# 128 instead of 96 stationary columns in the matmuls of an expert layer, and its bias in four groups of 32 rows

## The chip, the cores and the metric

The kernel runs on one core of a Trainium2 chip. The metric is device time in microseconds (us) of one execution, from the first to the last instruction plus what little lies around them; lower is better. The engines are TensorE (PE, with its weight loads listed apart as PEld), VectorE (DVE), ScalarE (ACT), GpSimd (POOL) and SyncE (SP), which here only issues DMAs.

## The reference

One encoder layer on 512 tokens of width 1024 in float32: three attention mixers with gates, then a mixture of experts with 32 experts of which each token takes four, then a final norm. The change touches the experts alone. What they compute, cut to what matters:

```
def expert_block(args):
    xb, e = args
    gu = xb @ w_gu[e] + b_gu[e]                       # 1024 -> 2048
    g = jnp.minimum(gu[:, :D_EXPERT], SWIGLU_LIMIT)
    lin = jnp.clip(gu[:, D_EXPERT:], -SWIGLU_LIMIT, SWIGLU_LIMIT)
    act = g * jax.nn.sigmoid(SWIGLU_ALPHA * g) * (lin + 1.0)
    return act @ w_down[e] + b_down[e]                # 1024 -> 1024
```

## The kernel before, in words

**Precision.** Large products are made of float32 values split in two fp32r parts, high and low. `A @ B` is then three matmuls: high x high, low x high, high x low.

**First part (0 to about 424 us).** Norm, projection, attention, gates and the output product. Its products (`gemm`, whose matmuls are recorded at L1440 to L1442) hold 128x128 stationary tiles and stream 512 columns. Then the router picks experts, and the 2048 token choices are packed into jobs. A job is one expert and up to 96 slots (`SLOTS = 96`); there are 32 jobs in this execution.

**Job loop (about 433 to 1580 us).** Each job has two products. `gate_up` has 8 weight parts of 1 MB; for each, 12 matmuls with the tokens' transposed chunk `xt_hi[:, k, :]` or `xt_lo[:, k, :]` (128 rows, 96 columns) as stationary operand and 512 columns of weights streaming into PSUM banks 0 to 3 (L1743 with the high weights `h_w`, L1746 with the low ones `l_w`). `down` has 4 weight parts, with 12 matmuls each, from `at_hi` and `at_lo` into banks 4 and 5 (L1761, L1766). Every matmul loads its stationary operand anew. So a job has 96 + 48 = 144 such matmuls. Between them stand 8 transposes of the activation (`turn_act`, in the second part of the next job's `gate_up`), 8 of the tokens to come (`turn_tokens`, after the first part of `down`), both recorded at L1467, and the bias.

**The bias of the first matrix.** It opens `gate_up` with four matmuls (L1735), one for each bank: a stationary operand `expert_gu` [96, 96] in bf16 that is one in the rows of the job's expert, and `bias_gu` [96, 2048] in bf16, which holds the bias of the 32 experts as three bf16 parts in three groups of 32 rows. POOL makes these parts after the attention (L941 to L959), and the first job's `expert_gu` just before that job (L992, L994); later ones are written by ACT (L839).

**Who feeds whom.** The parts of weights pass through 12 buffers `a_w`. SP loads a part when TensorE is through with the part 12 before it (L591, L594). ACT rounds `a_w` to `h_w` (L817; 8 buffers, so it waits for the part 8 before), and DVE subtracts to get `l_w` (L1190), in the buffer of `a_w`. DVE also makes `xt_lo` (L1329) and `at_lo` (L1334) and does most of the activation. The jobs' experts are read from a table, and the loop runs over pairs of jobs. The order on each engine is written out by hand; semaphores tie the engines.

**End.** `down_biases` (L1814) adds the second matrix' bias in float32, its stationary operand `gate_t` taken in groups of 32 rows; `last_rows` (L1818) adds the last job's rows with the 128-column stationary operands `token_hot`.

Of the kernel before, what the change touches and what calls it, by code (L numbers as in the profile page):

```python
# [102 lines left out]
def encoder_kernel(nc, x, mem, norm_mix, w_in, q_norm_a, k_norm_a, sink_b, norm_mem, w_mem_kv,  # L103
# [3 lines left out]
    with ctx:  # L107
# [40 lines left out]
        bias_f = sb("bias_f", [96, D], F32, 188 * KIB)  # L148
# [49 lines left out]
        bias_gu = sb("bias_gu", [96, 2 * D], BF16, 202 * KIB)  # L198
# [27 lines left out]
        blocks_end = small("blocks_end", [P, 3, N_EXP], F32)  # L226
        blocks_start = small("blocks_start", [P, 3, N_EXP], F32)
        job_ge = small("job_ge", [96, NJ], F32)
        job_lt = small("job_lt", [96, NJ], F32)
        job_hot = small("job_hot", [96, NJ], F32)  # L230
# [26 lines left out]
        at_hi = sb("at_hi", [P, KD, SLOTS], F32R, 174 * KIB)  # L257
        at_lo = sb("at_lo", [P, KD, SLOTS], F32R, 177 * KIB)
# [16 lines left out]
        job_hot_b = small("job_hot_b", [96, NJ], BF16)  # L275
        expert_gu = small("expert_gu", [96, SLOTS], BF16)
# [378 lines left out]
        def _(act):  # L655
# [181 lines left out]
            def name_gu(j):  # L837

                nc.scalar.activation(expert_gu[:], job_hot_b[:, bass.ds(j, 1)].to_broadcast([96, SLOTS]), ACT.Copy).then_inc(expert_gu_ready, 1)  # L839

            def take_xt(j):
                act.wait_ge(x_ps, j + 1)
                nc.scalar.activation(xt_hi[:].rearrange("p (h k) m -> p h (k m)", h=2), of_two_banks(6), ACT.Copy).then_inc(xt_hi_done, 1)

            def take_act(j):
                act.wait_ge(at_ps, j + 1)
                nc.scalar.activation(at_hi[:].rearrange("p (h k) m -> p h (k m)", h=2), of_two_banks(6), ACT.Copy).then_inc(at_hi_done, 1)
# [86 lines left out]
        def _(pool):  # L934
# [6 lines left out]
            bias_pieces = [(bias_gu[:, 0:D], b_gate_up[0][:, 0:D]), (bias_gu[:, D:2 * D], b_gate_up[0][:, D:2 * D])]  # L941
            pool.wait_ge(y_ps, STEPS)
            for n, (part, bias) in enumerate(bias_pieces):
                for g in range(3):
                    pool.dma_start(bias_f[N_EXP * g:N_EXP * (g + 1), :], bias).then_inc(bias_in, 16)
                pool.wait_ge(bias_in, 48 * (n + 1))

                def to_parts(rows):
                    step.link(nc.gpsimd.tensor_copy(part[rows, :], bias_f[rows, :]))

                def take_off(rows):
                    step.link(nc.gpsimd.tensor_tensor(bias_f[rows, :], bias_f[rows, :], part[rows, :], ALU.subtract))

                to_parts(slice(0, 96))
                for lo in (32, 64):
                    take_off(slice(lo, lo + 32))
                    to_parts(slice(lo, lo + 32))
                take_off(slice(64, 96))
                to_parts(slice(64, 96))  # L959
# [85 lines left out]
        def _(dve):  # L1045
# [230 lines left out]
            for g in range(3):  # L1276
# [4 lines left out]
            dve.wait_ge(blocks_ready, 3)  # L1281
# [4 lines left out]
            step.inc(nc.vector.tensor_tensor(job_ge[:], counter[0:96, 0:NJ], ps[0:96, 1, P:P + NJ], ALU.is_ge))  # L1286
# [574 lines left out]
```

## Time and profile before

| | |
|---|---|
| time, median of 3 runs | 1604.47 us (1602.7 to 1605.66) |
| time of the profiled execution | 1600.28 us |
| its span, first to last instruction | 1598.4 us |
| mean granted TensorE clock | 0.997 of 2.4 GHz |
| PE busy | 1566.0 us, 98% of the span |
| DVE busy | 1283.4 us, 80% |
| ACT busy | 1084.7 us, 68% |
| POOL busy | 432.0 us, 27% |

Busy time of PE is made of matmuls whose ends are modelled and overlap, so how fast it goes is read from the starts of matmuls, not from their durations. A row of the timeline that ends in x4 stands for four instructions in a row; the next row's start minus its own, divided by four, is the spacing. "Idle before" is time an engine had nothing to run, with what it waited for.

### The profile page before, as it was taken

To read this page: it belongs to the slowest core of one execution; us is meant where nothing else is said; L and a number is where in the kernel's file an instruction comes from. 1 tells how busy PE (TensorE), PEld (TensorE's weight loads), DVE (VectorE), ACT (ScalarE), POOL (GpSimd) and SP (SyncE) were. 2 spreads that over 40 slices of the span, in tenths; PEclk is the share of its full clock that TensorE was granted. 3 is DMA by queue.
4 is the path that set the end of the run, shared out by engine and by line. 5 is a ranking of instruction groups with operands and counts; after the bars stand their busy time and mean duration, and the time that the engine had idled before them with its cause. 6 is when DMAs were issued, how large, how long until landed. Compare 5 with 4: busy or idle time off the path is not lost.

```text
span 1598.4 us, 21810 instructions
## 1 busy us (share of the span) xinstructions
PE 1566.0 (98%) x7654; PEld 1139.1 (71%) x7654; DVE 1283.4 (80%) x1019; ACT 1084.7 (68%) x999; POOL 432.0 (27%) x265
## 2 busy tenths in 40 slices
PE   8999999999899999999999999999999999999997
PEld 7866688888766777777777777777777777777774
DVE  3768734337699989999898899998988999999984
ACT  6368723224477778777777787777777877777772
POOL 0000260000033622324432222344332223443220
PEclk9999999999999999999999999999999999999999
DMA  7310022337399999999999999999999999999983
GB/s 270 111 59 21 11 86 84 128 119 290 122 381 346 365 367 379 368 369 376 358 369 370 370 381 368 372 369 360 367 369 372 363 377 368 368 363 373 375 298 125
DMA packets 102566, 466.97 MB, mean 292 GB/s; under 512 B 13289, under 2 KB 13825, under 8 KB 69729
## 3 DMA queue, kind: packets, MB, share of 16 engines
q1 hardware_dynamic: 94416, 448.71, 73.5%
q0 software_dynamic: 7776, 17.68, 5.2%
q8 instruction: 24, 0.39, 0.1%
q10 hardware_dynamic: 336, 0.08, 0.0%
q14 instruction: 14, 0.11, 0.0%
HBM read 456.82 MB, written 19.27 MB: 298 GB/s over the span
## 4 chain that ended last, share of the span: by engine, by line
PE 91%; DVE 6%; issue 1%; DMA 1%; ACT 0%; POOL 0%; DVEq 0%; ACTq 0%; POOLq 0%
PE ps L1743 28%; PE ps L1761 14%; PE ps L1746 14%; PE ps L1766 7%; PE ps L1440 6%; PE ps L1442 6%; PE ps L1441 6%; PE ps L1467 4%; DVE l_w L1190 2%; PE ps L1735 2%; PE ps L1593 1%; DVE head_max L1119 1%; PE ps L1549 1%; DVE probs L1137 1%; PE ps L1476 0%
## 5 line engine op out<-in xcount | busy, mean ns | idle before, releaser
L1190 DVE TENSOR_TENSOR l_w<-a_w,h_w 128x2048 fp32r<-128x2048 f32 x384 | 865.4, 2290 | 31.0 <-ACT h_w L817 29.1
L817 ACT ACTIVATE h_w<-a_w 128x2048 fp32r<-128x2048 f32 x384 | 731.1, 1914 | 234.5 <-PE ps L1746 169.2
L965 POOL TENSOR_TENSOR mark_sb<-ones 1x1 f32<-1x1 f32 x93 | 245.9, 2644 | 718.6 <-ACT y_sb L865 708.5
L1743 PE MATMUL ps<-h_w,xt_hi 128*96 128x512 f32 x1024 | 286.7, 401 | 2.3 <-DVE xt_lo L1329 2.3
L1743 PE MATMUL ps<-h_w,xt_lo 128*96 128x512 f32 x1024 | 278.3, 393 | 0.0
L1746 PE MATMUL ps<-l_w,xt_hi 128*96 128x512 f32 x1024 | 277.9, 393 | 0.0
L1743 PEld LDWEIGHTS ps<-h_w,xt_lo 128*96 128x96 f32 x1024 | 165.6, 162 | 71.5
L1746 PEld LDWEIGHTS ps<-l_w,xt_hi 128*96 128x96 f32 x1024 | 165.2, 161 | 71.1
L1743 PEld LDWEIGHTS ps<-h_w,xt_hi 128*96 128x96 f32 x1024 | 163.3, 162 | 70.6 <-ACT h_w L817 1.7
L1761 PE MATMUL ps<-h_w,at_hi 128*96 128x512 f32 x512 | 162.1, 398 | 0.2 <-issue 0.2
L1761 PE MATMUL ps<-h_w,at_lo 128*96 128x512 f32 x512 | 159.5, 392 | 0.0
L486 DVE TENSOR_TENSOR w_low<-w_raw,w_high 128x2048 fp32r<-128x2048 f32 (+2 forms) x36 | 69.0, 1953 | 112.0 <-ACT w_high L478 112.0
L1766 PE MATMUL ps<-l_w,at_hi 128*96 128x512 f32 x512 | 139.0, 393 | 0.0
L1440 PE MATMUL ps<-w_high,h_hi 128*128 128x512 f32 x352 | 138.1, 392 | 0.6 <-DVE mem_lo L1065 0.5
L1442 PE MATMUL ps<-w_high,h_lo 128*128 128x512 f32 x352 | 137.1, 390 | 0.0
L1441 PE MATMUL ps<-w_low,h_hi 128*128 128x512 f32 x352 | 137.0, 389 | 0.0
L1761 PEld LDWEIGHTS ps<-h_w,at_lo 128*96 128x96 f32 x512 | 82.6, 161 | 36.1
L1766 PEld LDWEIGHTS ps<-l_w,at_hi 128*96 128x96 f32 x512 | 82.6, 161 | 35.9
L1761 PEld LDWEIGHTS ps<-h_w,at_hi 128*96 128x96 f32 x512 | 80.2, 162 | 32.1 <-issue 1.0
L971 POOL DMA_INDIRECT xg<-h_rows,gather_row x32 | 88.0, 2749 | 7.1 <-issue 5.4
L785 ACT ACTIVATE gate_sb<-ps,row_rstd 128x512 f32<-128x512 f32 x24 | 16.6, 690 | 105.7 <-PE ps L1442 105.7
L1440 PEld LDWEIGHTS ps<-w_high,h_hi 128*128 128x128 f32 x352 | 66.1, 188 | 15.1 <-DVE mem_lo L1065 0.8
(247 smaller groups left out, 1555.6 us busy)
## 6 DMA issues: line engine op xcount, KB each, us to landing
a_w<-in_w_gate_up SPq DMA_DIRECT2D x256, 1024.0 KB, 7.0
a_w<-in_w_down SPq DMA_DIRECT2D x128, 1024.0 KB, 6.6
w_raw<-in_w_in SPq DMA_DIRECT2D x8, 2048.0 KB, 8.0
w_raw<-in_w_out SPq DMA_DIRECT2D x2, 2048.0 KB, 7.6
w_raw<-in_w_in SPq DMA_DIRECT2D x2, 1024.0 KB, 7.8
x_sb<-in_x SPq DMA_DIRECT2D x8, 256.0 KB, 7.3
w_raw<-in_w_mem_kv SPq DMA_DIRECT2D x1, 2048.0 KB, 11.2
x<-in_x SPq DMA_DIRECT2D x4, 512.0 KB, 5.2
```

The lines of the kernel that those rows point to most:

```text
L486: nc.vector.tensor_tensor(wl[u % 2][:, a * COLS:b * COLS], raw[u % 2][:, a * COLS:b * COLS], wh[u % 2][:, a * COLS:b * COLS].bitcast(F32), ...
L817: nc.scalar.activation(h_w[m % H_SLOTS][:], a_w[m % A_SLOTS][:], ACT.Copy).then_inc(wh_done, 1)
L965: nc.gpsimd.tensor_tensor(mark_sb[:], ones[0:1, 0:1], ones[0:1, 0:1], ALU.mult).then_inc(marked, 1)
L971: nc.gpsimd.indirect_dma_start(out=xg[s][:], out_offset=None, in_=h2_rows, in_offset=bass.IndirectOffsetOnAxis(ap=rows, axis=0), bounds_ch ...
L1190: nc.vector.tensor_tensor(l_w[m % A_SLOTS][:], a_w[m % A_SLOTS][:], h_w[m % H_SLOTS][:].bitcast(F32), ALU.subtract).then_inc(wl_done, 1)
L1440: nc.tensor.matmul(bank, hi, w_hi, start=start, stop=False)
L1441: nc.tensor.matmul(bank, hi, w_lo, start=False, stop=False)
L1442: return nc.tensor.matmul(bank, lo, w_hi, start=False, stop=stop)
L1743: nc.tensor.matmul(ps[0:SLOTS, n, :], x_part[:, k, :], w_h[:, n * COLS:(n + 1) * COLS], start=False, stop=False)
L1746: last = nc.tensor.matmul(ps[0:SLOTS, n, :], xt_hi[:, k, :], w_l[:, n * COLS:(n + 1) * COLS], start=False, stop=k == KD - 1)
L1761: nc.tensor.matmul(ps[0:SLOTS, 4 + n, :], a_part[:, 2 * q + k, :], w_h[:, (2 * k + n) * COLS:(2 * k + n + 1) * COLS], start=q == 0 and k = ...
L1766: last = nc.tensor.matmul(ps[0:SLOTS, 4 + n, :], at_hi[:, 2 * q + k, :], w_l[:, (2 * k + n) * COLS:(2 * k + n + 1) * COLS], start=False, s ...
```

## The change

Every stationary operand of the job loop's matmuls gets 128 columns. A helper, `chunk`, takes them from a tile in which high and low part lie one after the other (`xt`, `at_both`): the 96 columns of chunk k and the first 32 of what follows it. The matmul writes all 128 partitions of its bank; partitions 96 to 127 hold sums that nobody reads, as the readers still take `ps[0:SLOTS]`. Only the very last chunk of the low part has nothing behind it, and stays at 96 columns (4 matmuls a job in `gate_up`, 2 in `down`). The bias becomes two fp32r tiles [128, 512], high and low, in which row group n (32 experts) holds the columns of bank n; `expert_gu` is [128, 128] in fp32r, and each bank takes one matmul of 32 rows from each tile: eight matmuls instead of four. Some preparing steps go from three groups to four.

```
-        bias_f = sb("bias_f", [96, D], F32, 188 * KIB)
+        bias_f = sb("bias_f", [P, COLS], F32, 188 * KIB)
-        bias_gu = sb("bias_gu", [96, 2 * D], BF16, 202 * KIB)
+        bias_hi = sb("bias_hi", [P, COLS], F32R, 202 * KIB)
+        bias_lo = sb("bias_lo", [P, COLS], F32R, 204 * KIB)
-        xt_hi = sb("xt_hi", [P, KD, SLOTS], F32R, 160 * KIB)
-        xt_lo = sb("xt_lo", [P, KD, SLOTS], F32R, 163 * KIB)
+        xt = sb("xt", [P, 2, KD * SLOTS], F32R, 160 * KIB)
+        xt_hi, xt_lo = (xt[:, n, :].rearrange("p (k m) -> p k m", k=KD) for n in range(2))
...
-        expert_gu = small("expert_gu", [96, SLOTS], BF16)
+        expert_gu = small("expert_gu", [P, P], F32R)
...
-            for n, (part, bias) in enumerate(bias_pieces):
-                for g in range(3):
-                    pool.dma_start(bias_f[N_EXP * g:N_EXP * (g + 1), :], bias).then_inc(bias_in, 16)
-                pool.wait_ge(bias_in, 48 * (n + 1))
...
+            for n in range(4):
+                pool.dma_start(bias_f[N_EXP * n:N_EXP * (n + 1), :], b_gate_up[0][:, n * COLS:(n + 1) * COLS]).then_inc(bias_in, 16)
+            pool.wait_ge(bias_in, 64)
+            step.link(nc.gpsimd.tensor_copy(bias_hi[:], bias_f[:]))
+            step.link(nc.gpsimd.tensor_tensor(bias_lo[:], bias_f[:], bias_hi[:].bitcast(F32), ALU.subtract))
...
-            step.link(nc.gpsimd.memset(expert_gu[:], 0.0))
-            for g in range(3):
-                nc.gpsimd.memset(expert_gu[N_EXP * g:N_EXP * g + 1, :], 1.0).then_inc(first_expert, 1)
-            pool.wait_ge(first_expert, 3)
+            step.link(nc.gpsimd.memset(expert_gu[:].bitcast(F32), 0.0))
+            for n in range(4):
+                nc.gpsimd.memset(expert_gu[N_EXP * n:N_EXP * n + 1, :].bitcast(F32), 1.0).then_inc(first_expert, 1)
+            pool.wait_ge(first_expert, 4)
...
-            for g in range(3):
+            for g in range(TB):
                 step.inc(nc.vector.tensor_tensor_scan(blocks_end[:, g, :], ones[:, 0:N_EXP], blocks[:], 0.0, ALU.mult, ALU.add))
...
+            def chunk(both, part, k):
+
+                w = SLOTS if part and k == KD - 1 else P
+                at = (part * KD + k) * SLOTS
+                return both[:].rearrange("p a m -> p (a m)")[:, at:at + w], w
...
-                for n in range(4):
-                    nc.tensor.matmul(ps[0:SLOTS, n, :], expert_gu[:], bias_gu[:, n * COLS:(n + 1) * COLS], start=True, stop=False)
+                for part in (bias_hi, bias_lo):
+                    for n in range(4):
+                        rows = slice(N_EXP * n, N_EXP * (n + 1))
+                        nc.tensor.matmul(ps[:, n, :], expert_gu[rows, :], part[rows, :], start=part is bias_hi, stop=False)
...
-                    for x_part in (xt_hi, xt_lo):
+                    for part in range(2):
+                        x_part, rows = chunk(xt, part, k)
                         for n in range(4):
-                            nc.tensor.matmul(ps[0:SLOTS, n, :], x_part[:, k, :], w_h[:, n * COLS:(n + 1) * COLS], start=False, stop=False)
+                            nc.tensor.matmul(ps[0:rows, n, :], x_part, w_h[:, n * COLS:(n + 1) * COLS], start=False, stop=False)
                     wait_low(pe, i, m)
                     for n in range(4):
-                        last = nc.tensor.matmul(ps[0:SLOTS, n, :], xt_hi[:, k, :], w_l[:, n * COLS:(n + 1) * COLS], start=False, stop=k == KD - 1)
+                        last = nc.tensor.matmul(ps[:, n, :], chunk(xt, 0, k)[0], w_l[:, n * COLS:(n + 1) * COLS], start=False, stop=k == KD - 1)
```

`down` is changed as `gate_up` is. Two places are shown as the engines' programs have them. The first is on TensorE, in the loop's body, at the seam where a `down` ends and the next `gate_up` begins with its bias. A number behind a name is its buffer; the last figures are the partitions and columns that are written. Before:

```order
L1761 MATMUL ps<-h_w_179,at_hi 96x512 x2
L1761 MATMUL ps<-h_w_179,at_lo 96x512 x2
L1766 MATMUL ps<-l_w_171,at_hi 96x512 x4
L1733 REGISTER_ALU
L1735 MATMUL ps<-bias_gu,expert_gu 96x512 x4
L534 REGISTER_ALU
L1743 MATMUL ps<-h_w_180,xt_hi 96x512 x4
L1743 MATMUL ps<-h_w_180,xt_lo 96x512 x4
```

And the same place of the changed kernel (high and low part are now one tile, so both read `at_both` or `xt`):

```order
L1759 MATMUL ps<-h_w_180,at_both 128x512 x6
L1759 MATMUL ps<-h_w_180,at_both 96x512 x2
L1764 MATMUL ps<-l_w_172,at_both 128x512 x4
L1727 REGISTER_ALU
L1731 MATMUL ps<-bias_hi,expert_gu 128x512 x4
L1731 MATMUL ps<-bias_lo,expert_gu 128x512 x4
L535 REGISTER_ALU
L1740 MATMUL ps<-h_w_181,xt 128x512 x8
L1743 MATMUL ps<-l_w_173,xt 128x512 x4
```

Nothing moved: the bias' four matmuls became eight, and all but the last two of the high weights' eight write 128 partitions.

The second place is on POOL, just ahead of the first gathering of tokens for the job loop (`xg` is the tile of gathered tokens, `h_rows` the rows in memory). Before:

```order
L987 MEMSET mark_sb 1x1
L989 MEMSET xg_186 96x1024
L989 MEMSET xg_187 96x1024
L992 MEMSET expert_gu 96x96
L994 MEMSET expert_gu 1x96 x3
L971 DMA xg_186<-h_rows,gather_row 96x1024
```

After:

```order
L975 MEMSET mark_sb 1x1
L977 MEMSET xg_186 96x1024
L977 MEMSET xg_187 96x1024
L980 MEMSET expert_gu 128x128
L982 MEMSET expert_gu 1x128 x4
L959 DMA xg_186<-h_rows,gather_row 96x1024
```

The gathering stands behind one memset more, and the first of them is larger.

## Rows read from the trace of the kernel before

**Rows 1.** Busy us (count): PE, PEld, DVE, ACT, POOL; then clock, DMA share, GB/s
```profile
520.00:1540.00 1020.00, 1020.00 (x4721) 719.56 (x4720) 924.75 (x491) 794.43 (x547) 357.01 (x204) 1.00 0.99 369
```

**Rows 2.** Waits in 600 to 1400 us: total, times, longest
```profile
SPq L591 <- PE ps L1746: 396.2, 179, 2.8
```

**Rows 3.** The chain that ended last: start, length, what
```profile
1204.26 1.85 PE ps L1761 x8
1239.72 1.85 PE ps L1761 x8
```

**Rows 4.** Timeline of PE around the first `gate_up` product within the loop
```profile
504.03 1.16 PE L1743 MATMUL ps<-h_w,xt_hi 128*96 128x512 f32 x4 [1.28 <-DVE xt_lo L1329]
```

**Rows 5.** Timeline of PE in the job loop: start, length, what
```profile
903.13 1.09 PE L1743 MATMUL ps<-h_w,xt_hi 128*96 128x512 f32 x4
...
916.07 1.09 PE L1746 MATMUL ps<-l_w,xt_hi 128*96 128x512 f32 x4
...
927.82 1.09 PE L1766 MATMUL ps<-l_w,at_hi 128*96 128x512 f32 x4
928.75 1.03 PE L1735 MATMUL ps<-bias_gu,expert_gu 96*96 96x512 bf16 x4
...
930.54 1.08 PE L1743 MATMUL ps<-h_w,xt_lo 128*96 128x512 f32 x4
```

**Rows 6.** Timeline of PE in the first part's products
```profile
257.78 0.39 PE L1442 MATMUL ps<-w_high,h_lo 128*128 128x512 f32 x1
...
261.86 0.39 PE L1442 MATMUL ps<-w_high,h_lo 128*128 128x512 f32 x1
...
377.08 0.40 PE L1441 MATMUL ps<-w_low,h_hi 128*128 128x512 f32 x1
...
378.70 0.39 PE L1442 MATMUL ps<-w_high,h_lo 128*128 128x512 f32 x1
...
379.38 0.39 PE L1442 MATMUL ps<-w_high,h_lo 128*128 128x512 f32 x1
```

**Rows 7.** Timeline of PE at the end of the kernel
```profile
1572.12 0.62 PE L1761 MATMUL ps<-h_w,at_hi 128*96 128x512 f32 x2
...
1579.53 1.09 PE L1766 MATMUL ps<-l_w,at_hi 128*96 128x512 f32 x4
1580.54 1.98 PE L1814 MATMUL ps<-down_bias,gate_t 32*128 32x512 f32 x4
1582.45 1.66 PE L1818 MATMUL ps<-y_hi_last,token_hot 96*128 96x512 f32 x6
1583.95 1.52 PE L1818 MATMUL ps<-y_lo_last,token_hot 96*128 96x512 f32 x6
```

**Rows 8.** Weight loads by form: count, busy us, mean ns, idle before
```profile
L1743 PEld LDWEIGHTS ps<-h_w,xt_hi 128*96 128x96 f32 x1024 | 163.3, 162 | 70.6 <-ACT h_w L817 1.7 <-DVE xt_lo L1329 1.5 <-issue 0.2
L1440 PEld LDWEIGHTS ps<-w_high,h_hi 128*128 128x128 f32 x352 | 66.1, 188 | 15.1 <-DVE mem_lo L1065 0.8 <-DVE h_lo L1160 0.3 <-issue 0.2
```

**Rows 9.** Timeline around `down_biases((0, 1))`: PE, and the weight loads
```profile
1566.11 1.09 PE L1766 MATMUL ps<-l_w,at_hi 128*96 128x512 f32 x4
1567.13 1.99 PE L1814 MATMUL ps<-down_bias,gate_t 32*128 32x512 f32 x8
1567.13 0.30 PEld L1814 LDWEIGHTS ps<-down_bias,gate_t 32*128 32x128 f32 x4 [0.39 <-issue]
1567.66 0.19 PEld L1814 LDWEIGHTS ps<-down_bias,gate_t 32*128 32x128 f32 x2 [0.24 <-issue]
1568.09 0.19 PEld L1814 LDWEIGHTS ps<-down_bias,gate_t 32*128 32x128 f32 x2 [0.24 <-issue]
```

**Rows 10.** Timeline of POOL and PE ahead of the job loop
```profile
427.32 0.62 POOL L994 MEMSET expert_gu<- 1x96 bf16 x3
428.84 1.04 POOL L971 DMA_INDIRECT xg<-h_rows,gather_row  x1 [0.90 <-POOL expert_gu L994]
433.02 0.88 PE L1467 MATMUL ps<-ident,xg 96*128 96x96 f32 x8 [1.50 <-DMA xg<-h_rows,gather_row]
```

More of the change, by code:

```diff
@@ L225, in encoder_kernel @@
         blocks = small("blocks", [P, N_EXP], F32)
[L226 to L230, printed above, removed]
+        blocks_end = small("blocks_end", [P, TB, N_EXP], F32)
+        blocks_start = small("blocks_start", [P, TB, N_EXP], F32)
+        job_ge = small("job_ge", [P, NJ], F32)
+        job_lt = small("job_lt", [P, NJ], F32)
+        job_hot = small("job_hot", [P, NJ], F32)
         place = small("place", [P, TB, N_EXP], F32)
@@ L251, in encoder_kernel @@
         h_w = [sb(f"h_w{i}", [P, 2 * D], F32R, at * KIB) for i, at in enumerate((0, 8, 16, 24, 128, 136, 112, 120))]
-        xt_hi = sb("xt_hi", [P, KD, SLOTS], F32R, 160 * KIB)
-        xt_lo = sb("xt_lo", [P, KD, SLOTS], F32R, 163 * KIB)
+        xt = sb("xt", [P, 2, KD * SLOTS], F32R, 160 * KIB)
+        xt_hi, xt_lo = (xt[:, n, :].rearrange("p (k m) -> p k m", k=KD) for n in range(2))
         xg = [sb(f"xg{i}", [SLOTS, D], F32, (166 + 4 * i) * KIB) for i in range(2)]
-        at_hi = sb("at_hi", [P, KD, SLOTS], F32R, 174 * KIB)
-        at_lo = sb("at_lo", [P, KD, SLOTS], F32R, 177 * KIB)
+        at_both = sb("at_both", [P, 2, KD * SLOTS], F32R, 174 * KIB)
+        at_hi, at_lo = (at_both[:, n, :].rearrange("p (k m) -> p k m", k=KD) for n in range(2))
         sg_sb = sb("sg_sb", [SLOTS, D], F32, 180 * KIB)
@@ L837, in name_gu @@
             def name_gu(j):
[L839 removed]
+                nc.scalar.activation(expert_gu[:], job_hot_b[:, bass.ds(j, 1)].to_broadcast([P, P]), ACT.Copy).then_inc(expert_gu_ready, 1)
             def take_xt(j):
                 act.wait_ge(x_ps, j + 1)
[L843 removed]
+                nc.scalar.activation(xt_hi.rearrange("p (h k) m -> p h (k m)", h=2), of_two_banks(6), ACT.Copy).then_inc(xt_hi_done, 1)
             def take_act(j):
                 act.wait_ge(at_ps, j + 1)
[L847 removed]
+                nc.scalar.activation(at_hi.rearrange("p (h k) m -> p h (k m)", h=2), of_two_banks(6), ACT.Copy).then_inc(at_hi_done, 1)
             def sigmoid(j, between=None):
@@ L1272, in _ @@
             step.link(nc.vector.tensor_scalar(blocks[:, 0:1], blocks[:, 0:1], 1.0, None, ALU.max))
-            for g in range(3):
+            for g in range(TB):
                 step.inc(nc.vector.tensor_tensor_scan(blocks_end[:, g, :], ones[:, 0:N_EXP], blocks[:], 0.0, ALU.mult, ALU.add))
             dve.wait_ge(dve_chain, step.n)
-            for g in range(3):
+            for g in range(TB):
                 nc.vector.tensor_tensor(blocks_start[:, g, :], blocks_end[:, g, :], blocks[:], ALU.subtract).then_inc(blocks_ready, 1)
             step.inc(nc.vector.tensor_scalar(job_table[0:1, 1, 1:2], blocks_end[0:1, 0, N_EXP - 1:N_EXP], 0.5, -0.75, ALU.mult, ALU.add))
-            dve.wait_ge(blocks_ready, 3)
+            dve.wait_ge(blocks_ready, TB)
             step.link(nc.vector.scalar_tensor_tensor(out=place[:], in0=blocks_start[:, 0:1, :].to_broadcast([P, TB, N_EXP]), scalar=float(SLOTS),
@@ L1758, in down @@
                     for k in range(2):
-                        for a_part in (at_hi, at_lo):
+                        for part in range(2):
+                            a_part, rows = chunk(at_both, part, 2 * q + k)
                             for n in range(2):
-                                nc.tensor.matmul(ps[0:SLOTS, 4 + n, :], a_part[:, 2 * q + k, :], w_h[:, (2 * k + n) * COLS:(2 * k + n + 1) * COLS],
-                                                 start=q == 0 and k == 0 and a_part is at_hi, stop=False)
+                                nc.tensor.matmul(ps[0:rows, 4 + n, :], a_part, w_h[:, (2 * k + n) * COLS:(2 * k + n + 1) * COLS],
+                                                 start=q == 0 and k == 0 and part == 0, stop=False)
                     wait_low(pe, i, m)
@@ L1765, in down @@
                         for n in range(2):
-                            last = nc.tensor.matmul(ps[0:SLOTS, 4 + n, :], at_hi[:, 2 * q + k, :], w_l[:, (2 * k + n) * COLS:(2 * k + n + 1) * COLS],
+                            last = nc.tensor.matmul(ps[:, 4 + n, :], chunk(at_both, 0, 2 * q + k)[0], w_l[:, (2 * k + n) * COLS:(2 * k + n + 1) * COLS],
                                                     start=False, stop=q == DN_PARTS - 1 and k == 1)
```

27 lines of the change are left out of this document (8 added, 19 removed).

## The prediction

> **What bounds the kernel now.** I read the stretches first. From 520 to 1540 us TensorE is busy all of the time, at full clock, while DVE is busy 924.75 of 1020 us (91%), ACT 794 us (78%) and the DMA engines nearly always (0.99, 369 GB/s) [rows 1]. Three candidates, then: PE, DVE and DMA. The waits decide against DMA: SP, which issues the loads, waited 396 us of the 800 from 600 to 1400 for TensorE to free a buffer, and for the `gate_up` parts alone [rows 2]. Loads are held back by PE, not PE by loads. The chain that ended last shows PE repeating itself every 35.46 us (1239.72 - 1204.26) [rows 3]; that is one job. DVE needs 0.907 x 35.46 = 32.2 us of it, ACT 27.6 us. So PE sets the pace from 504 us on. Before that it does not: at 504.03 it still waits 1.28 us for DVE's `xt_lo` [rows 4], since DVE is catching up with its `l_w` there. What PE saves in the first two jobs is lost in that wait; about 30.5 of the 32 jobs count (30 whole ones and the last `down`).
>
> How fast PE goes is read from starts. From 903.13 to 916.07 us there are 14 groups of four: 12.94 / 56 = 231.1 ns a matmul, with 96 stationary columns and 512 streamed [rows 5]. In the first part of the kernel the same kind of matmul, fp32r, 512 streamed columns, a new weight load each, but 128 stationary columns, starts every 4.08 / 18 = 226.7 ns (257.78 to 261.86) [rows 6]. So a wider stationary operand goes with a shorter spacing, by 4.4 ns.
>
> Is it the columns? The two stages differ in other things. First, DVE, ACT and DMA work beside the job loop. But the last `down` keeps 7.41 / 32 = 231.6 ns from 1572.12 to 1579.53, when the loads and the splitting of weights are over [rows 7]. Second, the job loop changes its bank with each matmul, while `gemm` stays in one. But the final matmuls L1818 (128 columns of `token_hot`) also change bank each time, and the six from 1583.95 last 1.52 us, which less the 0.39 us of one is 1.13 / 5 = 226 ns [rows 7]. What is left is the columns.
>
> The short spacing is not there at once. After transposes, `gemm` starts with seven at 1.62 / 7 = 231.4 ns (377.08 to 378.70) and only then goes to 0.68 / 3 = 226.7 ns [rows 6]. With 96 columns it doesn't come in 56 in a row [rows 5].
>
> **The change, part by part.**
>
> *The 144 matmuls of a job.* PE is disturbed at four places: bias, two sets of transposes, and the matmuls that stay at 96 columns. I take seven long spacings behind each of the first three (21), the 4 narrow ones in `gate_up` and seven behind them (11), the 2 narrow ones in `down` with the four up to the next bias (6): 38 keep 231 ns and 106 gain 4.3 ns. That is -0.456 us a job. Bounds: all 144 gain, -0.62 us; none, 0.
>
> *Longer weight loads.* A load of 128 columns takes 188 ns, one of 96 takes 162 [rows 8]. In a stream it is covered by the matmul before it (over 220 ns). Where a full operand is loaded behind transposes, which last under 100 ns each, it isn't: 26 ns twice a job, +0.05 us. Bounds 0 and +0.1.
>
> *The bias.* Now, from 927.82 to 930.54 us there are four L1766, the four bias matmuls and four L1743: 2.72 us, and less eight at 0.231 the bias costs 0.87 us a job [rows 5]. After: eight matmuls, each of 32 rows, in four row groups of the array. No row shows fp32r in this form; the nearest is `down_biases` in float32. With one row group, two matmuls (four records, since float32 takes two each) last 1.98 us [rows 7]; with two row groups, four matmuls (eight records) last 1.99 us, and their loads come in twos, four loads of about 0.18 us within 0.30 us [rows 9]. So different row groups run beside each other. With four groups I expect two rounds of 0.227 us and some 0.02 for their staggered starts, 0.48 us. But such a switch costs time. On the way in, 1.02 us pass from 1566.11 to 1567.13 for four matmuls that take 0.92: +0.10 [rows 9]. Within the form, a float32 round takes 0.43 us (loads at 1567.66 and 1568.09 [rows 9]); from 1580.54 to 1582.45 there are four rounds, 1.72 us, but 1.91 us pass: +0.19, a first load that nothing covers and a drain at the end [rows 7]. And the six L1818 from 1582.45 take 1.50 instead of 1.36 us: +0.14, of which 0.03 are the long first spacings that I counted already [rows 7]. Together 0.48 + 0.10 + 0.19 + 0.11 = 0.88 us, and for two more groups' loads at the start I take 0.91: +0.04 us a job. Bounds: no switching cost, 0.48 - 0.87 = -0.39; no overlap of the row groups, 8 x 0.227 + 0.43 - 0.87 = +1.38 (with all the switching).
>
> On weight loads the Trainium skill speaks against this form ("TensorE: Matmul & The Clock Gate", LDWEIGHTS): the time goes by the columns, P / 1.2 ns, so 32 rows cost as much as 128. The durations agree in slope (32 columns more, 26 ns more [rows 8]). Eight loads of 128 columns in a row would by that page be an estimated 0.85 us, as much as the old bias in all; but it also says that loads of different row groups overlap, and [rows 9] show it for two.
>
> *Ahead of the loop.* POOL writes the first `expert_gu` (three memsets, 0.62 us together) and then gathers the first tokens, for which PE waits 1.50 us [rows 10]. One memset more (0.2 us) and a larger first one (128x128 float32 for 96x96 bf16) put the gathering back by 0.3 us, and nothing takes it up, as DVE and PE both start from it. One more scan and one more subtraction on DVE lie beside this wait. +0.3 us once. Bounds 0 and 0.6.
>
> *At nothing:* making the bias' parts, on POOL, shorter than before and long ahead of its first use; SP waits for it only ahead of loads that wait for the merging too. If that cover were gone it would be a gain. ACT writes a larger `expert_gu` (0.3 us of ACT, which has 7.9 us a job free). The partitions 96 to 127 written in vain cost no streamed column. DVE, DMA and ACT do what they did; a job of 35.1 instead of 35.46 us asks 1% more of each, and DVE's 32.2 us fit.
>
> **Sum.** A job: -0.456 + 0.05 + 0.04 = -0.37 us. Times 30.5: -11.2 us; with +0.3 us: -10.9 us. The profiled execution, 1600.28 us, would come to 1589.4 us; it ran 4.2 us under the median of the runs shown, so against that 1604.47 the forecast is 1593.5 us. From no change this measurement can tell about 0.2%, 3.2 us.
>
> **The rivals.**
>
> *The short spacing never comes in the job loop.* The seven long spacings behind each disturbance are there, and something that I did not see keeps the others long too. Then 0.05 + 0.04 = +0.09 us a job and +0.3: +3 us, 1607.5 us. For it: L1818 shows only five short spacings with changing banks. Against: nothing else differs.
>
> The Trainium skill would have this (same page, Back-to-back issue gap): N / 2.4 + 2.5 ns, 215.8 ns for 512 streamed columns, whatever the stationary operand has. The trace disagrees, with 231.1 and 226.7 ns [rows 5, 6].
>
> *The four row groups do not overlap.* This is the other side. Place: the eight bias matmuls at the head of each `gate_up`. Price +1.38 us a job instead of +0.04, so 30.5 x (-0.456 + 0.05 + 1.38) = +29.7 us, 1634 us. It decides from the point where the bias takes 0.41 us more than now (1.28 us). For it: two groups were seen, never four, and never in fp32r. Against: [rows 9]. Overlap by halves, two and two, would be 0.93 us with 0.43, +0.49 a job, +3 us in all, within the first rival's range.
>
> *Switching costs nothing.* The loads of a 32-row group are hidden as others are, -0.39 us a job: 30.5 x (-0.456 + 0.05 - 0.39) = -24.3 us, 1580.5 us. For it: the four matmuls ahead of the present bias, which has 96 of 128 rows, pass in 0.93 us, without a gap [rows 5]. Against: each switch to 32 rows in [rows 7, 9].
>
> *DMA becomes the bound.* The engines are at 0.99, and the gain would stop where it begins: 1604 us. Against: [rows 2].
>
> **How the numbers follow.** Forecast 0.58, with its own range 1586 to 1600 us (all matmuls gain, or half of the 106); never short, or two and two, 0.17, about 1607; no overlap 0.09, 1634; switching free 0.13, 1580; DMA 0.03. Leaving out the 1634 case and the far ends of the others, the range is 1579 to 1608 us. Faster: 0.58 + 0.13 = 0.71. Same: half of the 0.17 case and more, and DMA, 0.15. Slower: 0.14.
>
> **What would show it.** In the changed kernel's timeline of the job loop: spacings near 226.7 ns from the eighth matmul behind transposes on (if 231 stays, the first rival); one job shorter than 35.46 by about 0.37 us; from the last `down` group's start to the second group of `gate_up`, 2.76 instead of 2.72 us (4.1: no overlap; 2.3: free switching); the matmuls at 96 columns followed by some of 231 ns; PE's wait ahead of the first transposes later by 0.3 us. The sum would be wrong above all if the narrow matmuls disturb nothing (then nearer -0.45 us), or if with four groups the switch costs other than with two.

## The result, and the profile after

The changed kernel is slower: 1610.56 us (median of 6 runs, 1609.28 to 1611.8) against 1603.93 us for the kernel before beside it (6 runs, 1602.49 to 1605.66), a ratio of 1.0043 with an interval of 1.0032 to 1.0054. The forecast was 1593.5 us and faster. The profiled execution of the changed kernel took 1609.7 us, with a span of 1607.9 us.

The page's busy times and the job loop's stretch in the changed kernel (busy us and count of PE, PEld, DVE, ACT, POOL; then clock, DMA share, GB/s), beside [rows 1]:

```profile
PE 1575.7 (98%) x7782; PEld 1253.5 (78%) x7782; DVE 1278.7 (80%) x1021; ACT 1085.7 (68%) x999; POOL 394.6 (25%) x252
520.00:1540.00 1020.00, 1020.00 (x4805) 814.17 (x4804) 919.93 (x488) 791.68 (x543) 347.38 (x203) 1.00 0.98 368
```

The waits of 600 to 1400 us, beside [rows 2] (total, times, longest):

```profile
SPq L592 <- PE ps L1743: 393.1, 177, 2.9
```

And the chain of work that ended last, beside [rows 3] (start, length, what):

```profile
1140.39 1.90 PE ps L1759 x8
...
1176.02 1.90 PE ps L1759 x8
```

The structure is the same: in this stretch PE is never idle and runs at full clock, and SP waits for it as long as before. But DVE, ACT and DMA do a little less in the same stretch, since a job now takes 1176.02 - 1140.39 = 35.63 us instead of 35.46. From the starts of all complete jobs between 600 and 1500 us the means are 35.644 us (25 jobs) and 35.460 us (26 jobs of before): +0.184 us, times 30.5 jobs +5.6 us. So the loss lies inside the jobs, on PE.

The timeline of PE in the changed kernel, the same stretch of a `gate_up` as [rows 5] (start, length, what):

```profile
909.03 2.03 PE L1740 MATMUL ps<-h_w,xt 128*128 128x512 f32 x8
910.90 1.09 PE L1743 MATMUL ps<-l_w,xt 128*128 128x512 f32 x4
911.83 2.01 PE L1740 MATMUL ps<-h_w,xt 128*128 128x512 f32 x8
913.67 1.08 PE L1743 MATMUL ps<-l_w,xt 128*128 128x512 f32 x4
914.58 2.03 PE L1740 MATMUL ps<-h_w,xt 128*128 128x512 f32 x8
916.45 1.09 PE L1743 MATMUL ps<-l_w,xt 128*128 128x512 f32 x4
917.38 2.01 PE L1740 MATMUL ps<-h_w,xt 128*128 128x512 f32 x8
```

A weight part is 12 matmuls. The part from 909.03 takes 2.80 us (233 ns a matmul), the next 2.75 (229), the next 2.80 again (233). All have 128 columns. They alternate with the number of the chunk: these are k = 3, 4 and 5. The short spacing was to come from the eighth matmul on and stay; here it comes in every second part and is lost again. The single spacings, as means over the complete jobs of each trace (my own reckoning from the starts, in ns, in order):

```
changed, k odd  (3, 5):  241 232 231 232 228 230 232 241 232 231 232 233   sum 2796
changed, k even (4, 6):  236 224 231 236 228 232 231 227 227 227 227 232   sum 2757
before,  k odd  (3, 5):  230 236 228 232 230 236 228 232 230 236 228 232   sum 2779
before,  k even (4, 6):  228 229 231 232 228 229 231 232 228 229 231 233   sum 2761
```

Two things were in the trace of before, too, and I had not looked: a pattern that repeats every four matmuls, and that differs between odd and even chunks. Its timeline shows it in the parts k = 4 (from 905.91 us, 2.76 us) and k = 5 (from 908.67 us, 2.78 us):

```profile
905.91 1.08 PE L1743 MATMUL ps<-h_w,xt_hi 128*96 128x512 f32 x4
...
908.67 1.09 PE L1743 MATMUL ps<-h_w,xt_hi 128*96 128x512 f32 x4
...
911.45 1.08 PE L1743 MATMUL ps<-h_w,xt_hi 128*96 128x512 f32 x4
```

The mean of 231.1 ns in [rows 5] hides both.

The two profiles differ by 9.5 us in span, the medians by 6.6. Part of the rest is the granted clock: the changed kernel's profiled execution had it at 0.50 from 420.6 to 427.4 us and from 437.6 to 441.0 us, where that of before had 1.00. It isn't the change: the profile of run 6 below, which has the old bias and 96 columns, had 0.51 in the first of these stretches, and that of run 10, with the new bias, 1.00.

### The profile page after: what moved, and what is told of

Its sections match the earlier page's. It is cut to its first block, busy times and chain, and to the rows that moved or that the text cites. A ratio compares the mean times of both kernels' runs of the same rounds, so it can differ in the third digit from the quotient of the medians.

```text
span 1607.9 us, 22055 instructions
## 1 busy us (share of the span) xinstructions
PE 1575.7 (98%) x7782; PEld 1253.5 (78%) x7782; DVE 1278.7 (80%) x1021; ACT 1085.7 (68%) x999; POOL 394.6 (25%) x252
## 4 chain that ended last, share of the span: by engine, by line
PE 92%; DVE 5%; issue 1%; DMA 1%; ACT 0%; DVEq 0%; ACTq 0%; POOLq 0%
PE ps L1740 29%; PE ps L1759 14%; PE ps L1743 14%; PE ps L1764 7%; PE ps L1428 6%; PE ps L1430 6%; PE ps L1429 6%; PE ps L1455 4%; PE ps L1731 1%; DVE l_w L1178 1%; PE ps L1581 1%; DVE head_max L1107 1%; PE ps L1537 1%; DVE probs L1125 1%; PE ps L1658 1%
## 5 line engine op out<-in xcount | busy, mean ns | idle before, releaser
L1740 PE MATMUL ps<-h_w,xt 128*128 128x512 f32 (+1 forms) x2048 | 525.1, 398 | 3.1 <-DVE xt L1317 3.1
L1740 PEld LDWEIGHTS ps<-h_w,xt 128*128 128x128 f32 (+1 forms) x2048 | 378.7, 187 | 102.2 <-issue 11.5
L1743 PE MATMUL ps<-l_w,xt 128*128 128x512 f32 x1024 | 277.6, 393 | 0.0
L1759 PE MATMUL ps<-h_w,at_both 128*128 128x512 f32 (+1 forms) x1024 | 261.4, 397 | 0.2 <-issue 0.2
L1743 PEld LDWEIGHTS ps<-l_w,xt 128*128 128x128 f32 x1024 | 192.8, 188 | 44.2
L1759 PEld LDWEIGHTS ps<-h_w,at_both 128*128 128x128 f32 (+1 forms) x1024 | 188.6, 187 | 44.8 <-issue 1.0
L1764 PE MATMUL ps<-l_w,at_both 128*128 128x512 f32 x512 | 140.8, 397 | 0.0
L1764 PEld LDWEIGHTS ps<-l_w,at_both 128*128 128x128 f32 x512 | 96.4, 188 | 23.5
L1430 PEld LDWEIGHTS ps<-w_high,h_lo 128*128 128x128 f32 x352 | 66.1, 188 | 13.8
L1429 PEld LDWEIGHTS ps<-w_low,h_hi 128*128 128x128 f32 x352 | 66.1, 188 | 13.3
```

The costliest lines, as they stand in the source:

```text
L1429: nc.tensor.matmul(bank, hi, w_lo, start=False, stop=False)
L1430: return nc.tensor.matmul(bank, lo, w_hi, start=False, stop=stop)
L1740: nc.tensor.matmul(ps[0:rows, n, :], x_part, w_h[:, n * COLS:(n + 1) * COLS], start=False, stop=False)
L1743: last = nc.tensor.matmul(ps[:, n, :], chunk(xt, 0, k)[0], w_l[:, n * COLS:(n + 1) * COLS], start=False, stop=k == KD - 1)
L1759: nc.tensor.matmul(ps[0:rows, 4 + n, :], a_part, w_h[:, (2 * k + n) * COLS:(2 * k + n + 1) * COLS], start=q == 0 and k == 0 and part == 0, ...
L1764: last = nc.tensor.matmul(ps[:, 4 + n, :], chunk(at_both, 0, 2 * q + k)[0], w_l[:, (2 * k + n) * COLS:(2 * k + n + 1) * COLS], start=False ...
```

## Experiments

All ratios are against the kernel before, run beside the experiment. "Job" is the mean period of complete jobs between 600 and 1500 us of the profiled execution; before has 35.460 us. Bytes are counted from the start of the tile that holds the stationary operand.

The first question was what differs between odd and even chunks. In the changed kernel chunk k starts at 384 k bytes (96 columns of 4 bytes) and ends 512 bytes further on. So an even k ends at a multiple of 256 bytes, an odd one 128 bytes past one. Theory A: the place of the stationary operand in its tile sets the spacing. Theory B: the register arithmetic and the waits between the weight parts do. Rival C: the spacing is a side matter and the new bias makes the loss. I first took the start of the operand for the place that counts, and runs 1 and 4 were forecast by it. After run 4 there were two forms of A: A1, only the end counts; A2, start and end do.

### 1. The same 128 columns, taken from a multiple of 512 bytes

It multiplies by other columns of the tile than the right ones, and by just as many.

```
                 at = (part * KD + k) * SLOTS
+                at = at // 128 * 128
```

> The changed kernel, but each 128-column stationary operand of the job loop is read from the nearest lower multiple of 128 columns of its tile (so it multiplies by other columns than it should; only the place of the reads differs). Theory A (what disturbs the matmuls is where in SBUF the stationary operand starts: chunks of 96 columns begin at multiples of 384 bytes, and the parts with odd k, whose start is no multiple of 256 bytes, are those with spacings of 241 ns): the odd parts look like the even ones, 12 matmuls in 2757 ns instead of 2796, and a job comes to about 35.4 us or less instead of 35.64; if the settled 226.7 ns is then kept across the parts too, 35.1 us. Theory B (register arithmetic and register waits at the seam between parts disturb them): nothing changes, 35.64 us.

Measured: 1591.7 us (5 runs), ratio 0.993 [0.9917, 0.9943], a job 35.077 us. Nearly all spacings are 227 ns; longer ones are left in the last chunk, whose operand with the low part keeps 96 columns, and behind the bias and one set of transposes (ten and nine of them). The number of columns, the bias, the waits and the register arithmetic stayed, so this is theory A, and the gain that the forecast had named is there: -0.38 us a job, beside -0.37 forecast. That the same columns are now read more than once is a rival that run 8 settles.

### 2. The old bias with 128 columns

The changed kernel with the bias of before: bf16, three groups, four matmuls. Only its stationary operand is widened to 128 columns.

```
-        expert_gu = small("expert_gu", [P, P], F32R)
+        expert_gu = small("expert_gu", [96, P], BF16)
...
+                for n in range(4):
+                    nc.tensor.matmul(ps[:, n, :], expert_gu[:], bias_gu[:, n * COLS:(n + 1) * COLS], start=True, stop=False)
```

> 128 columns in the products, but the bias as before (four bf16 matmuls of 96 rows). Theory A and B alike: the bias block cost the same before and after (1330 ns from the last matmul ahead of it to the second one behind it, less two ordinary spacings), so a job stays at 35.64 us within 0.1 us, and the time within 3 us of the changed kernel's. Rival C (the eight 32-row matmuls are what made the kernel slower): a job goes back to 35.46 us, and the time to that of the kernel before.

Measured: 1608.0 us (8 runs), ratio 1.0037 [1.0023, 1.0051], a job 35.633 us, with the same pattern (241 233 231 232 at the head of the odd parts). The loss stays without the new bias.

### 3. The loop written out on PE

```
-            with pe.Fori(0, pairs_but_one) as i:
+            for i in range(15):
```

> The changed kernel with TensorE's loop over 15 pairs of jobs written out, so that its waits are on constants and no register arithmetic stands between the parts (the other engines keep their loops). Theory B: the disturbances at the seams go, most matmuls start every 226.7 ns, a job comes to 35.1 us, and the kernel is faster than before by 10 us. Theory A: the pattern by odd and even k stays, 35.64 us a job, no change in time.

Measured: 1608.46 us (5 runs), ratio 1.0035 [1.0022, 1.0047], a job 35.644 us. PE's timeline:

```profile
907.11 2.03 PE L1740 MATMUL ps<-h_w,xt 128*128 128x512 f32 x8
...
909.90 2.01 PE L1740 MATMUL ps<-h_w,xt 128*128 128x512 f32 x8
...
912.66 2.03 PE L1740 MATMUL ps<-h_w,xt 128*128 128x512 f32 x8
```

Again 2.79 and 2.76 us, with the loop's register arithmetic gone. Theory B falls.

### 4. Five forms in the first part of the kernel

The products of the first part stay in one bank, have no loop and little beside them. The kernel before, whose gate products take stationary operands of other width and place, for some output blocks u and the middle k. Their results are other values.

```
+        FORMS = {6: (96, 0), 8: (96, 32), 10: (P, 32), 12: (P, 64), 14: (96, 64)}
...
+                            hi_m, lo_m = (v[:].rearrange("p k m -> p (k m)")[:, at:at + w] for v in (hi, lo))
+                            last = three(ps[0:w, BANK[u] + t, :], hi_m, lo_m, h_w[:, k, :], l_w[:, k, :], False, False)
```

> The kernel before, with other forms of the stationary operand in the gate products of the first part, one form for each product (k = 1 to 6; other columns than it should, so the values differ): 128 columns starting at a multiple of 512 bytes (control), 96 columns at 512, 96 at 512 + 128 bytes, 128 at 512 + 128, 128 at 512 + 256, 96 at 512 + 256. There are no registers here and few waits. Theory A: 226.7 ns for the control and for 512 + 256, about 231 ns for starts at 512 + 128, whatever the width. If it is the width: 231 ns for the three with 96 columns. Theory B: 226.7 ns for all six.

PE's timeline, one stretch of nine spacings for each of four forms:

```profile
218.51 0.39 PE L1442 MATMUL ps<-w_high,h_hi 128*96 128x512 f32 x1
...
220.58 0.39 PE L1442 MATMUL ps<-w_high,h_hi 128*96 128x512 f32 x1
...
248.74 0.39 PE L1442 MATMUL ps<-w_high,h_hi 128*96 128x512 f32 x1
...
250.78 0.39 PE L1442 MATMUL ps<-w_high,h_hi 128*96 128x512 f32 x1
...
275.95 0.40 PE L1442 MATMUL ps<-w_high,h_hi 128*128 128x512 f32 x1
...
278.05 0.39 PE L1442 MATMUL ps<-w_high,h_hi 128*128 128x512 f32 x1
...
306.34 0.39 PE L1442 MATMUL ps<-w_high,h_hi 128*128 128x512 f32 x1
...
308.38 0.39 PE L1442 MATMUL ps<-w_high,h_hi 128*128 128x512 f32 x1
```

2.07, 2.04, 2.10 and 2.04 us for nine. The first and the last of a block's eight chunks (k = 0 and 7) keep the ordinary operand; the means here are of the 17 spacings between the 18 matmuls of k = 1 to 6 alone, over the blocks of each form:

```
columns  starts at  ends at (bytes past a multiple of 512)   spacing, ns
   96        0        384                                      230.0
   96      128          0                                      226.7
   96      256        128                                      230.0
  128      128        128                                      232.8
  128      256        256                                      226.7
```

The expectation, which went by the start, missed all three forms with 96 columns (short for 0 and 256, long for 128) and had the two with 128 right; by the width alone the second and the fourth would have been missed.

With 96 columns the spacing can be 226.7 ns, and with 128 it can be 232.8. It is short where the end is at a multiple of 256 bytes, though starts differ (128, 256, and 0 in the ordinary form of [rows 6]). That speaks for A1; A2 can't say why 96 columns from 128 bytes on are fast.

### 5. The kernel before, with 96 columns that begin at multiples of 512 bytes

It takes other columns than the right ones; each operand ends 128 bytes past a multiple of 256.

> The kernel before, 96 columns, each stationary operand starting at a multiple of 512 bytes and ending 384 bytes past it (other columns than it should). A1: no short spacings, 230.0 ns in the steady state, as in the forms run, and a job near 35.35 us. If it is the start that counts: 226.7 ns and 35.0 us.

Measured: 1599.05 us (10 runs), ratio 0.9973 [0.9963, 0.9983], a job 35.327 us. In the steady state the spacings are 231 232 228 229, mean 230.0: never 226.7, although each operand starts well aligned. So the even chunks of the kernel before, which end 384 bytes past a multiple of 768, have what their end asks for (2761 / 12 = 230.1). Its odd chunks end at a multiple of 256 and yet have 231.6; runs 6 and 7 bear on that.

### 6. The kernel before, with 96 columns that end at multiples of 512 bytes

```
+            def aligned(tile, k):
+                at = k * SLOTS // 128 * 128 + 32
+                return tile[:].rearrange("p k m -> p (k m)")[:, at:at + SLOTS]
```

> The kernel before, 96 columns, but each stationary operand starts 128 bytes past a multiple of 512 bytes and so ends at one (other columns than it should). A1: 226.7 ns between most matmuls, a job near 35.0 us, 0.99 of before. A2: 231 ns as before, 35.46 us.

Measured: 1591.59 us (4 runs), ratio 0.9923 [0.9903, 0.9943], a job 35.033 us. With 96 columns (again other ones) nearly the whole gain is there. PE's timeline, `gate_up` from the end of the activation's transposes on, and then `down` behind those of the tokens:

```profile
1005.22 1.13 PE L1747 MATMUL ps<-h_w,xt_hi 128*96 128x512 f32 x4
...
1008.01 1.07 PE L1747 MATMUL ps<-h_w,xt_hi 128*96 128x512 f32 x4
...
1018.89 1.07 PE L1747 MATMUL ps<-h_w,xt_hi 128*96 128x512 f32 x4
...
1024.33 0.82 PE L1467 MATMUL ps<-ident,xg 96*128 96x96 f32 x8
...
1026.85 1.09 PE L1770 MATMUL ps<-l_w,at_hi 128*96 128x512 f32 x4
...
1032.41 1.08 PE L1770 MATMUL ps<-l_w,at_hi 128*96 128x512 f32 x4
```

From 1008.01 to 1018.89 are 48 matmuls, 10.88 us, 226.7 ns. From 1026.85 to 1032.41, behind the tokens' transposes, are 24 in 5.56 us: 231.7 ns (230 236 228 233), with operands that end just as well, and it stays so to the end of `down`. That is the pattern of the odd chunks in the kernel before. Not every set of transposes brings it: behind those of the activation the second spacing is 227 ns already (1005.22 to 1008.01 are 2.79 us, one of 292 ns and eleven of 227). Behind those of the tokens the stream with 96 columns keeps it for all 36 matmuls that are left of `down`. A stream with 128 columns leaves it: after seven spacings in [rows 6], after nine at this place in run 8, and the changed kernel's even chunks after seven. That the odd chunks of the kernel before are slow by the same state, and come into it by the even ones ahead, is an inference from the like pattern, which run 7 supports.

### 7. Even chunks with 128 columns, odd ones with 96

The tiles of the changed kernel are kept. Now every operand ends at a multiple of 256 bytes, except the last chunk's with the low weights, which has 128 columns so that all rows of the bank are closed.

```
-                w = SLOTS if part and k == KD - 1 else P
+                w = P if k % 2 == 0 or close else SLOTS
```

> The changed kernel, with 128 columns only for the even chunks and 96 for the odd ones (128 again for the last low-weight matmuls of each product), so that each operand ends at a multiple of 256 bytes although the odd ones start 128 bytes off. Computes what the reference does. Theory A1 (it is the end of the operand that counts): nearly all matmuls at 226.7 ns, a job at 35.1 us, 0.993 of before. Theory A2 (both start and end have to be at multiples of 256 bytes): odd parts stay near 231 ns, a job about 35.4 us.

Measured: 1593.35 us (6 runs), ratio 0.994 [0.9922, 0.9957], a job 35.107 us. Spacings are 227 ns in even and odd parts alike. The exceptions are 241 233 231 232 in the closing matmuls that end 128 bytes off, ten spacings behind the bias and thirteen behind the tokens' transposes. An odd chunk begins 384 bytes past a multiple of 768, so begins as badly as before, and is fast: A1 holds, A2 falls. It is also the very operand of the kernel before, with 96 columns and the same place. There it has 231.6 ns and here 227, with fast even chunks ahead of it.

### 8. The chunks 128 columns apart

The changed kernel, with gaps of 32 columns between chunks (the tiles `xt` and `at_both` grow by 2 KiB each, POOL clears the gaps once, the readers and writers take strided views). Every operand then begins and ends at a multiple of 512 bytes, and all 144 have 128 columns.

```
+        xt = sb("xt", [P, 2, KD * P], F32R, 160 * KIB)
+        xt_hi, xt_lo = (xt[:, n, :].rearrange("p (k m) -> p k m", k=KD)[:, :, 0:SLOTS] for n in range(2))
...
+                return both[:, part, k * P:(k + 1) * P], P
```

> The changed kernel, with the chunks of xt and at_both 128 columns apart (512 bytes) instead of 96, so each chunk starts and ends at a multiple of 512 bytes; computes what the reference does. Theory A (the place of the stationary operand in its tile sets the spacing): as the run with rounded starts, nearly all matmuls at 226.7 ns, a job at about 35.1 us, time 0.993 of the kernel before. Rival: the gain with rounded starts came from reading the same columns again; then the spacing stays at 231 ns and the time at that of the changed kernel.

Measured: 1589.46 us (6 runs), ratio 0.9918 [0.9901, 0.9934]. It beats both kernels. Its timeline and its chain:

```profile
908.98 1.98 PE L1741 MATMUL ps<-h_w,xt 128*128 128x512 f32 x8
910.79 1.07 PE L1744 MATMUL ps<-l_w,xt 128*128 128x512 f32 x4
911.70 1.98 PE L1741 MATMUL ps<-h_w,xt 128*128 128x512 f32 x8
```

```profile
1127.99 1.87 PE ps L1760 x8
...
1162.99 1.87 PE ps L1760 x8
```

12 matmuls in 2.72 us, 226.7 ns; a job 35.00 us. Each operand has its own columns here, so the rival of run 1 falls. From the changed kernel it is -0.64 us a job. Run 1, which moves the reads alone, gives 0.57 of it; besides, this run has no narrow operand left, and other tiles stand elsewhere.

### 9. The same with the old bias

> Chunks 128 columns apart and operands of 128 columns, but the bias as before (four bf16 matmuls of 96 rows); computes what the reference does. The bias blocks cost 0.87 us a job in both forms, so a job at 35.0 us. With the new bias the ten matmuls behind it take 50 ns more than the short spacing in the run with chunks 128 apart, with the old one about 11 ns, which would make it 1 us faster at most, too little to be sure of; 0.992 of the kernel before. If the bias form mattered once the spacing is short, more than 0.1 us a job would show.

Measured: 1588.56 us (4 runs), ratio 0.9903 [0.9888, 0.9919], a job 34.987 us. The best figure, but not told apart from run 8.

### 10. The new bias alone, with 96 columns

> The new bias alone: eight matmuls of 32 rows, but all stationary operands with 96 columns as before. Theory A (the loss is from the 128-column operands of odd chunks, which end 128 bytes past a multiple of 256): a job at 35.46 to 35.50 us, no change in time that can be told (within 2 us of before). Rival C (the bias makes the loss): 35.64 us, +6 us.

Measured: 1600.8 us (12 runs), ratio 0.9986 [0.9977, 0.9996], a job 35.407 us, 0.05 less than before. That is a little less than the 35.46 to 35.50 expected. Rival C falls: the bias does not cost. With 96 columns the seam, from the last matmul ahead of the bias to the second one behind it, even takes 1.27 us, where it takes 1.33 in the kernels before and after. PE's timeline at the seam:

```profile
929.48 1.09 PE L1764 MATMUL ps<-l_w,at_both 128*96 128x512 f32 x4
930.50 0.48 PE L1731 MATMUL ps<-bias_hi,expert_gu 32*96 32x512 f32 x4
930.81 0.41 PE L1731 MATMUL ps<-bias_lo,expert_gu 32*96 32x512 f32 x4
931.14 2.09 PE L1740 MATMUL ps<-h_w,xt 128*96 128x512 f32 x8
933.07 1.09 PE L1743 MATMUL ps<-l_w,xt 128*96 128x512 f32 x4
```

### 11. Five more forms

As run 4, to try the rule at other widths.

```
+        FORMS = {6: (64, 0), 8: (64, 32), 10: (112, 16), 12: (112, 0), 14: (P, 16)}
```

> More forms of the stationary operand in the gate products of the first part, as in the first forms run (other columns than it should). The end rule: 64 columns from 0 (ends at 256 bytes): 226.7 ns; 64 columns from 128 bytes (ends at 384): about 230 ns; 112 columns from 64 bytes (ends at 512): 226.7 ns; 112 from 0 (ends at 448): above 226.7 ns; 128 columns from 64 bytes (ends at 576): above 226.7 ns. If it is the start together with the width, 112 columns from 64 bytes are as long as 128 from 64 bytes.

PE's timeline, nine spacings with 64 columns and nine with 112:

```profile
217.87 0.40 PE L1442 MATMUL ps<-w_high,h_hi 128*64 128x512 f32 x1
...
219.94 0.39 PE L1442 MATMUL ps<-w_high,h_hi 128*64 128x512 f32 x1
...
275.50 0.39 PE L1442 MATMUL ps<-w_high,h_hi 128*112 128x512 f32 x1
...
277.54 0.39 PE L1442 MATMUL ps<-w_high,h_hi 128*112 128x512 f32 x1
```

The means, taken as in run 4:

```
columns  starts at  ends at (bytes past a multiple of 512)   spacing, ns
  112       64          0                                      226.7
  112        0        448                                      229.1
  128       64         64                                      233.5
   64        0        256                                      230.0
   64      128        384                                      229.2
```

With 96, 112 and 128 columns the rule holds for every end that was tried: short only where it is at a multiple of 256 bytes. With 64 columns it doesn't: 230.0 ns where I expected 226.7. That was a miss, and why is open.

## Why the prediction was wrong

**"What is left is the columns."** This is the step that failed. I had 231.1 ns with 96 columns in the job loop and 226.7 with 128 in `gemm` [rows 5, 6], ruled out two other differences between the stages by rows, and took what remained for the cause. There was a third difference that I had not listed: `gemm` cuts its operands at multiples of 512 bytes, the job loop at multiples of 384. Runs 4 and 11 separate the two: 96 columns are fast with the right end, 128 are slow with a wrong one. The change widened the operands but left their starts 96 columns apart, so half of them end badly. Odd chunks became slower than before (2796 instead of 2779 ns for 12; 128 columns that end 128 bytes off have 232.8 ns in run 4, too), even ones hardly faster (2757 instead of 2761), as each has seven longer spacings behind the odd part ahead of it.

The final rows L1818 in [rows 7] were read rightly (226 ns at 128 columns), but they, too, end at multiples of 512 bytes, and so could not tell width from place. A comparison in which both differ at once is no evidence for either.

**The terms of the sum**, us a job:

```
                                           forecast   measured
144 matmuls' spacings                       -0.456     +0.13
  (the same with operands that end right, 8)           -0.51
weight loads behind the transposes          +0.05      +0.05
bias                                        +0.04       0.00
sum                                         -0.37      +0.184
  (with operands that end right, run 8)                -0.456
```

*Spacings.* +0.184 less 0.05 for the loads leaves +0.13; `gate_up`'s odd parts have 0.06 of it, `down`, which changes chunk twice in a part, 0.09, and the rest is -0.02. The size of the gain was rightly estimated for operands that end right: run 8 gets -0.456 - 0.05 = -0.51, somewhat more than -0.456, as there are no narrow matmuls left to disturb. (That run 8's whole job differs by -0.456 us, the figure of this term, is chance.) Where the long spacings stand was not foreseen, though: seven were to come behind each of the bias and the two sets of transposes, 21 in all. Run 8 has ten behind the bias, none behind the activation's transposes and nine behind those of the tokens, 19 in all, so that the total came out by luck.

*Weight loads.* The mean loads of the changed kernel (count, busy, mean ns, idle before):

```profile
L1740 PEld LDWEIGHTS ps<-h_w,xt 128*128 128x128 f32 x1920 | 358.1, 189 | 94.0 <-issue 11.5 <-ACT h_w L818 2.2 <-DVE xt L1317 1.7
```

27 ns more than in [rows 8], and the first spacing behind each set of transposes grew from 289 and 292 ns to 314 and 318: right.

*The bias.* PE's timeline of the changed kernel:

```profile
933.86 1.11 PE L1764 MATMUL ps<-l_w,at_both 128*128 128x512 f32 x4
934.89 0.51 PE L1731 MATMUL ps<-bias_hi,expert_gu 32*128 32x512 f32 x4
935.24 0.40 PE L1731 MATMUL ps<-bias_lo,expert_gu 32*128 32x512 f32 x4
935.56 2.10 PE L1740 MATMUL ps<-h_w,xt 128*128 128x512 f32 x8
937.50 1.08 PE L1743 MATMUL ps<-l_w,xt 128*128 128x512 f32 x4
```

From 933.86 to 937.50 pass 3.64 us; less 12 at 0.231 the bias costs 0.87 us, just what it cost before. The parts came out, too: +0.11 on the way in (forecast 0.10), 0.67 for the eight (0.48 + 0.19), +0.09 on the way out (0.11). Only the place within the form was wrong. I had put the 0.19 down to a first load and a drain, once; but the two rounds take 0.35 and 0.32 us, so each costs about 0.1 us more than the 0.227 I took. So the rivals "no overlap" (+1.38) and "switching free" (-0.39) were rightly given little. The four loads of a round, each of another row group, end within 0.19 us together:

```profile
934.89 0.19 PEld L1731 LDWEIGHTS ps<-bias_hi,expert_gu 32*128 32x128 f32 x4 [0.37 <-issue]
```

The Trainium skill has it that loads of different row groups overlap ("TensorE: Matmul & The Clock Gate", The mechanism). This trace agrees, for four groups now: 0.19 us is the time of a single load of 128 columns.

*Ahead of the loop.* The last POOL steps of the changed kernel:

```profile
426.87 0.21 POOL L980 MEMSET expert_gu<- 128x128 f32 x1
427.14 0.95 POOL L982 MEMSET expert_gu<- 1x128 f32 x4
430.64 1.03 POOL L959 DMA_INDIRECT xg<-h_rows,gather_row  x1 [2.54 <-DVE gather_row L1257]
```

In this execution DVE's `gather_row` ended the wait, and the memsets (0.21 + 0.95 = 1.16 us for 0.79) are hidden. `gather_row` starts at 429.54 us here and at 427.30 in the kernel before. It is as late (429.50) in run 6, which has nothing of the change and had a granted clock of 0.51 from 420.6 to 427.4 us, so I put it down to the clock. With full clock in that stretch the memsets are not hidden: in runs 1, 3 and 10 the gathering starts 1.92 us after `gather_row` does, in the kernel before and run 5, which have the old bias and 96 columns, 1.54 and 1.53. So +0.38 us where +0.3 was forecast.

*"DMA becomes the bound"*: run 8 shows it isn't; the loop ran 14 us faster with the same transfers.

**The rivals.** "The short spacing never comes in the job loop" (1607.5 us) was the nearest in time, and named "something that I did not see"; what it was, and that it can make spacings longer than before, I had no row for. I had put the chance of slower at 0.14 and the upper end at 1608. The Trainium skill's formula ("TensorE: Matmul & The Clock Gate", Back-to-back issue gap) gives 215.8 ns for 512 streamed columns and has no term for the stationary operand. The section offers it for a single isolated matmul and says that in a stream with a load for each matmul both set the spacing, so the prediction asked more of it than it states. Its number fits none of the fp32r forms measured (226.7 to 233.5 ns).

**In all**: +5.6 us from the jobs and about +0.4 ahead of the loop make 6.0 of the 6.6 us between the medians; the rest is within their uncertainty.

**Open**: why the end of the stationary operand matters; why 64 columns follow another rule; why the tokens' transposes are followed by long spacings and the activation's are not; and why a stream of 96 columns keeps the state of 231.7 ns there while one of 128 leaves it.

## What to carry to other kernels

Where a stream of fp32r matmuls reloads the stationary operand each time, look at the single spacings before the mean, and put operands of 96 to 128 columns so that each ends at a multiple of 256 bytes: here that is worth 0.6 to 1% of the whole kernel (runs 6 to 9), with 96 columns (run 6) about as much as with 128. Before a difference between two stages is put down to one property, list what else differs in the instruction's operands, place as well as shape, and try them apart in a spare stage: two runs with five forms each were enough for that. Padding the chunks to 128 columns (run 8) takes 4 KiB a partition and gave the shortest times, with either bias (runs 8 and 9).

## What the runs showed of the hardware

- fp32r matmuls, 512 streamed columns, a new load each: 226.7 ns with operands of 96, 112 or 128 columns that end at a multiple of 256 bytes of their tile (runs 4, 7, 8, 11); else 229.1 (112 columns), 230.0 (96), 232.8 and 233.5 (128). The start alone does not decide: 96 and 128 columns from the same start, 0 or 128 bytes, have different spacings.
- Behind the transposes of the tokens a stream with 128 columns has nine longer spacings and then 226.7 ns (run 8); one with 96 columns stays at 231.7 ns for all 36 matmuls to the end of `down` (run 6). Behind those of the activation both have 227 ns from the second spacing on.
- Eight matmuls of 32 rows in four row groups take 0.67 us (0.35 + 0.32), start to start, and 0.87 us with what they disturb, as much as four bf16 matmuls of 96 rows there (rows of the changed kernel and [rows 5]).
